# Forgetting branch, three of four head pairs: the second head's probabilities are turned through VectorE squares and DRAM too

## The chip, the cores and the metric

The kernel runs on one core of a Trainium2 chip. The metric is device time in microseconds (us) of one execution, as the median of three runs. One further execution was taken with the hardware profiler; the profile and the trace are of that one. Engines are named PE (TensorE), DVE (VectorE), ACT (ScalarE), POOL (GpSimd) and SP (SyncE). A line such as L1264 is line 1264 of the kernel before.

## What is computed

One layer of a decoder: an RMS norm, one input projection, three causal token mixers (A forgetting attention, B sparse attention with a top-k indexer, C dilated windows), each with its own gate, a merge, an output projection, the residual and a last norm. Sequence 1024, model width 1024, float32. The change touches mixer A (and, by a shared helper, a little of B's bookkeeping). Cut to A:

```
def forgetting_attention(q, k, v, log_f):
    scale = Dh ** -0.5
    c = jnp.cumsum(log_f, axis=1).transpose(0, 2, 1)
    ...
    def block(i):                      # 128 queries
        logits = jnp.einsum('bqhd,bkhd->bhqk', qb, k, preferred_element_type=F32) * scale
        logits = logits + (cb[..., :, None] - c[..., None, :])
        logits = jnp.where(kpos[None, :] <= qpos[:, None], logits, -jnp.inf)
        p = jax.nn.softmax(logits, axis=-1)
        return jnp.einsum('bhqk,bkhd->bqhd', p.astype(v.dtype), v)
```

A has 8 heads of 64 channels. A query block b (0 to 7) sees (b + 1) blocks of 128 keys.

## The kernel before

**Order of the work.** `build_plan` writes one list of steps by hand (kinds such as `logits`, `square`, `turn`, `exp`, `pv`, `block`). Each engine walks that same list and issues its own part of every step, in order, and semaphores tie the engines together. So what stands behind a waiting instruction in the list waits too, on that engine.

**Tiling of A.** Two heads make a chunk of 128 channels, the "channel" `ch` 0 to 3. In a channel the query blocks go in six runs: (0,1), (2,3), 4, 5, 6, 7, which see 3, 7, 5, 6, 7 and 8 key blocks of 128 for each head. `pair_run` lays the runs out as a pipeline over steps s:

1. `logits` of run s: PE multiplies queries by keys for both heads into PSUM slots (L1252); DVE adds the causal triangle and the forget bias and takes the row maximum (L1870, L1871).
2. `square` of run s (only where `by_dma` holds): ACT computes exp for the first head into `pa[:, 0]` (L1506). DVE transposes it in place with one STREAM_TRANSPOSE (L1792), which turns each 32 x 32 square of it but leaves the squares where they are.
3. `turn` of run s - 1: PE transposes what has not gone the other way, 128 x 128 at a time, against an identity (L1264), in groups of up to four to a PSUM bank; ACT copies each group to `pta` (L1537).
4. `exp` of run s: ACT computes exp for the second head (L1519), then issues the store of the first head's squares to a DRAM scratch (L1528). POOL issues four loads (L1036), one for each 32 partitions, which bring the squares back to where a full transpose has them, in one of the two tiles `ptsa`.
5. `pv` of an earlier run (3 steps back, `LAG`; 2 where the next run isn't `by_dma`): PE multiplies values by the turned probabilities of both heads (L1291), ACT copies the result to `ya` (L1554).
6. The rest of the step is filled with pieces of the next channel's projection, 12 matmuls of 512 columns a piece (`block`, L1118 to L1120). Two blocks of weights, with two such pieces each (one for each half of the 1024 tokens), make a tile q, k or v; when a half is done, ACT and DVE copy it out of its PSUM bank in two parts, high and low (`qa`, `ka`: L1483, L1814; `va`: L1805). Only then may PE claim that bank again.

`by_dma` holds in A for 17 of the 24 runs: all of channels 0 and 1 and all but the last of channel 2. In these 17 runs the first head goes through DVE and DRAM, the second through PE. The weights of a block go through SP's queue into `w_raw`, then ACT (L1355) and DVE (L1651) split them into `w_hl`, three blocks ahead. The two PSUM slots are freed by ACT's exps (`slot_free`); `logits` of a run wait for the slots of the run before.

**Places in time.** Channels 0 to 2 of A run from 611 to 774 us of the trace. The runs of channel 1 have their `logits` at 660.35, 671.93, 683.88, 693.35, 699.01 and 708.51 us.

## Time and profile before

| | us |
|---|---|
| median of 3 runs | 1348.44 (1348.2 to 1348.98) |
| the profiled execution itself | 1348.53 |
| its span, first to last instruction | 1346.7 |
| PE busy | 1326.0 (98%) |
| DVE busy | 771.0 (57%) |
| ACT busy | 629.4 (47%) |
| POOL busy | 264.1 (20%) |

The busy time of an engine is the union of its instructions; matmuls overlap one another, so a row's count times its mean is more than the time it takes on PE. What a group of matmuls takes is the distance from its start to the start of the next group. Idle time of an engine other than PE costs nothing by itself.

### The profile page before, as it was taken

To read this page: it belongs to the slowest core of one execution; us is meant where nothing else is said; L and a number is where in the kernel's file an instruction comes from. 1 tells how busy PE (TensorE), PEld (TensorE's weight loads), DVE (VectorE), ACT (ScalarE), POOL (GpSimd) and SP (SyncE) were. 2 spreads that over 40 slices of the span, in tenths; PEclk is the share of its full clock that TensorE was granted. 3 is DMA by queue.
4 is the path that set the end of the run, shared out by engine and by line. 5 is a ranking of instruction groups with operands and counts; after the bars stand their busy time and mean duration, and the time that the engine had idled before them with its cause. 6 is when DMAs were issued, how large, how long until landed. Compare 5 with 4: busy or idle time off the path is not lost.

```text
span 1346.7 us, 20780 instructions
## 1 busy us (share of the span) xinstructions
PE 1326.0 (98%) x7690; PEld 1082.1 (80%) x7690; DVE 771.0 (57%) x1716; ACT 629.4 (47%) x1381; POOL 264.1 (20%) x423
## 2 busy tenths in 40 slices
PE   7999999999999999999999999999999999999998
PEld 6988888777878888887788777787878788888886
DVE  6569866766766875565555555744445354233534
ACT  7467766766754541113443465644454322213223
POOL 3123211002103100003344313323332220000000
PEclk9999999999999999999999999999999999999999
DMA  7054222122214322225555423433544352222522
GB/s 227 24 141 126 71 63 72 50 53 73 72 41 119 99 64 82 80 72 163 162 153 155 141 87 105 127 92 84 156 127 124 119 161 55 78 78 63 188 100 96
DMA packets 146052, 139.54 MB, mean 104 GB/s; under 512 B 13888, under 2 KB 124096, under 8 KB 145696
## 3 DMA queue, kind: packets, MB, share of 16 engines
q0 software_dynamic: 22896, 67.42, 16.9%
q1 hardware_dynamic: 97824, 58.22, 16.0%
q10 hardware_dynamic: 25232, 12.59, 3.2%
q8 instruction: 62, 1.02, 0.3%
q14 instruction: 38, 0.31, 0.1%
HBM read 99.95 MB, written 34.03 MB: 99 GB/s over the span
## 4 chain that ended last, share of the span: by engine, by line
PE 95%; DVE 2%; ACT 1%; issue 1%; POOL 1%; DMA 0%; ACTq 0%; POOLq 0%; DVEq 0%
PE bank L1118 23%; PE bank L1120 23%; PE bank L1119 23%; PE bank L1291 6%; PE slot L1252 6%; PE bank L1264 5%; PE slot L1118 2%; PE slot L1119 2%; PE slot L1120 2%; PE slot L1226 1%; PE bank L1131 0%; DVE slot L1871 0%; ACT yc L1554 0%; DMA iq_st<-iq_hl 0%; PE bank L1177 0%
## 5 line engine op out<-in xcount | busy, mean ns | idle before, releaser
L1118 PE MATMUL bank<-hs,w_hl 128*128 128x512 f32 x1088 | 431.5, 397 | 0.7 <-DVE qa L1814 0.7
L1120 PE MATMUL bank<-hs,w_hl 128*128 128x512 f32 x1088 | 424.3, 390 | 0.0
L1119 PE MATMUL bank<-hs,w_hl 128*128 128x512 f32 x1088 | 423.8, 390 | 0.0
L1651 DVE TENSOR_TENSOR w_hl<-w_raw,w_hl 128x512 fp32r<-128x512 f32 (+1 forms) x168 | 113.6, 678 | 220.7 <-ACT w_hl L1355 219.2
L1120 PEld LDWEIGHTS bank<-hs,w_hl 128*128 128x128 f32 x1088 | 204.2, 188 | 44.0
L1118 PEld LDWEIGHTS bank<-hs,w_hl 128*128 128x128 f32 x1088 | 204.3, 188 | 43.6 <-issue 3.4
L1119 PEld LDWEIGHTS bank<-hs,w_hl 128*128 128x128 f32 x1088 | 204.6, 188 | 39.6
L1355 ACT ACTIVATE w_hl<-w_raw 128x512 fp32r<-128x512 f32 (+1 forms) x168 | 103.9, 621 | 165.1 <-PE bank L1120 155.9
L1678 DVE TENSOR_SCALAR_CACHE_REDUCE idle_out<-score,state 128x768 uint8<-128x768 f32 (+3 forms) x140 | 115.0, 822 | 4.0
L1871 DVE CUSTOM_DVE_ANT_0 slot<-slot,score 128x128 f32<-128x128 f32 (+5 forms) x64 | 47.0, 786 | 50.1 <-PE slot L1252 50.0
L1560 ACT ACTIVATE idle_out<-score,state 128x896 bf16<-128x896 f32 x64 | 69.9, 1093 | 10.0 <-DVE state L1674 8.8
L1036 POOL DMA_DIRECT2D ptsa<-square_scratch x68 | 48.3, 718 | 91.6 <-PE bank L1291 68.8
L1602 ACT ACTIVATE tm<-bank 128x512 f32<-128x512 f32 x46 | 27.5, 598 | 72.3 <-PE bank L1120 72.2
L1036 POOL DMA_DIRECT2D ptsb<-square_scratch x48 | 31.1, 654 | 79.4 <-DMA square_scratch<-pb 68.2
L1036 POOL DMA_DIRECT2D c_tables<-square_scratch x48 | 30.8, 648 | 65.9 <-DMA square_scratch<-pb 65.9
L1849 DVE SCALAR_TENSOR_TENSOR score<-relu_t,nat,score 128x1024 f32<-128x1024 f32 (+5 forms) x42 | 37.9, 947 | 5.0 <-ACT relu_t L1468 4.5
L1870 DVE TENSOR_TENSOR slot<-slot,tri_b 128x128 f32<-128x128 f32 x64 | 20.5, 320 | 33.7 <-PE slot L1252 33.1
L1519 ACT ACTIVATE share_b<-slot,c_tables 128x128 f32<-128x128 f32 (+1 forms) x96 | 38.6, 421 | 1.1 <-DVE c_tables L1871 0.9
L1871 DVE CUSTOM_DVE_ANT_0 slot<-slot,negc 128x128 f32<-128x128 f32 (+7 forms) x48 | 36.8, 766 | 1.7
L1291 PE MATMUL bank<-pta,va 128*64 128x128 f32 x376 | 36.6, 277 | 1.1 <-ACT pta L1537 1.1
L1554 ACT ACTIVATE yb<-bank 128x128 f32<-128x128 f32 (+1 forms) x24 | 7.5, 313 | 64.3 <-PE bank L1291 64.2
L1118 PE MATMUL bank<-ych,w_hl 128*128 128x512 f32 x96 | 37.3, 389 | 0.0
(338 smaller groups left out, 2415.1 us busy)
## 6 DMA issues: line engine op xcount, KB each, us to landing
w_raw<-in_w_in_dram SPq DMA_DIRECT2D x136, 256.0 KB, 2.9
merged_scratch<-ms POOLq DMA_DIRECT2D x16, 512.0 KB, 3.5
ms<-merged_scratch POOLq DMA_DIRECT2D x16, 512.0 KB, 4.0
square_scratch<-pb ACTq DMA_DIRECT2D x20, 256.0 KB, 2.3
xn<-in_x_dram SPq DMA_DIRECT2D x8, 512.0 KB, 6.6
iq_st<-iq_hl POOLq DMA_DIRECT2D x32, 128.0 KB, 2.8
w_raw<-in_w_o_dram SPq DMA_DIRECT2D x16, 256.0 KB, 4.0
v_scratch<-vtc POOLq DMA_DIRECT2D x6, 512.0 KB, 3.1
```

Of the source, the lines that this page charges most:

```text
L1036: pool.dma_start(PTQ[br][n % 2][32 * j:32 * j + 32, 0:W // P, :].rearrange("a b (i c) -> a (b i) c", i=4), mid[0:W // P, :, 32 * j:32 * j ...
L1118: pe.matmul(out_, wh, mh, start=start, stop=False)
L1119: pe.matmul(out_, wh, ml, start=False, stop=False)
L1120: return pe.matmul(out_, wl, mh, start=False, stop=stop)
L1252: ins = pe.matmul(slot_of(a, hh)[1][:, c0:c1], qt[qp][rows, tq], kt[kp][rows, first + c0:first + c1], start=n == 0, stop=n == 2)
L1264: ins = pe.transpose(bank[grp["use"][0]][:, j * P:(j + 1) * P], PR[u["br"]][:, row, at_col:at_col + P], ident[:])
L1291: ins = pe.matmul(bank[a["pv"][0]][cols, out], values, turned, start=c == 0, stop=c == n - 1)
L1355: A(dst, src, ACTF.Copy).then_inc(w_high, 1)
L1560: A(idle_out[:, 0:W], score_of(j + 2), ACTF.Sign, bias=cand[:, j:j + 1].bitcast(F32), scale=-1.0, accum_out=val[:, j:j + 1]).then_inc(act_ ...
L1651: v.tensor_tensor(lo, src, hi.bitcast(F32), ALU.subtract).then_inc(w_low, 1)
L1678: return v.tensor_scalar(idle_out8[:, 0:W] if W <= 6 * P else idle_out[:, 0:W], score_of(j + 2), cand[:, j:j + 1].bitcast(F32), None, op, ...
L1871: v.tensor_tensor_reduce(o, o, logit_bias(x, hh), -slope, 0.0, ALU.add, ALU.min, stats_of(x, hh)[0]).then_inc(logit_ready, 1)
```

## The change

In the 17 `by_dma` runs of A the second head goes the way of the first:

- `HEADS` says how many heads go through squares: 2 in A, 1 in B. `moved` now holds both heads' blocks, so `turn` has no groups for these runs.
- A new step `square_second` stands right behind `exp`: DVE transposes `pa[:, 1]` in place, waiting for ACT's exp of it, and ACT issues its store, waiting for that transpose.
- POOL issues the same four loads a run, each now of both heads' blocks, and waits for both stores.
- ACT's exp of the second head waits until the second store of the run before has landed (`second_stored`), since the store reads `pa[:, 1]`.
- The `ptsa` tiles are twice as large (16 blocks of 128, 8 KiB a partition) and lie at 36 and 44 KiB, the first of them where `pta` is; the first run that turns by PE again waits until the last `pv` from that tile is done. One `negc` tile moves from 48 to 76 KiB. There are four DRAM scratches instead of two, each twice as large.

The diff:

```diff
@@ -57,2 +57,3 @@
 SQUARED = {"a": 8, "b": 4}
+HEADS = {"c": 1, "a": 2, "b": 1}
 LAG = {"a": 3, "b": 2}
@@ -77,3 +78,3 @@
     count = {"ring": 0, "tp": 0, "hs": 0, "S": 0, "L": 0, "unit": 0, "z": 0, "zt": 0, "qk": 0, "taken": 0}
-    tiles, unit_of_tp, units_seen, last_split, last_taken, squares = {}, [], [], {}, {}, []
+    tiles, unit_of_tp, units_seen, last_split, last_taken, squares, goals = {}, [], [], {}, {}, [], [0, 0]
 
@@ -273,3 +274,5 @@
                     return
-                own = [(x["b"], 0, c) for x in runs[s] for c in range(x["W"] // P)]
+                own = [[(x["b"], hh, c) for x in runs[s] for c in range(x["W"] // P)] for hh in range(HEADS[br])]
+                goal, second = goals[len(squares) % 2], sum(y["br"] == "a" for y in squares)
+                goals[len(squares) % 2] += 64
                 at = len(squares) - 2
@@ -277,3 +280,4 @@
                     x.update(square=len(squares), single=sum(y["slots"] == 1 for y in squares),
-                             moved={part: k for k, part in enumerate(own[:SQUARED[br]])})
+                             moved={part: k for k, part in enumerate(part for parts in own for part in parts[:SQUARED[br]])},
+                             wide=min(len(own[0]), SQUARED[br]) * P, room=squares[-4]["goal"] if len(squares) > 3 else 0, goal=goal + 64, second=second)
                 step("square", unit=runs[s][-1], n=len(squares), before=squares[at] if at >= 0 else None)
@@ -303,2 +307,7 @@
                 plan.append(("exp", runs[s][-1]))
+                if by_dma[s] and br == "a":
+                    step("square_second", unit=runs[s][-1])
+                elif br == "a":
+                    for x in runs[s]:
+                        x["behind"] = squares[-1]
             x = runs[min(s, n - 1)][-1]
@@ -629,3 +638,3 @@
         PT = {br: at(k, f"pt{br}", [P, PTS[br], 4, P]) for br, k in (("c", 54), ("a", 36), ("b", 40))}
-        PTQ = {"a": [at(k, f"ptsa{k}", [P, TB, P]) for k in (44, 76)], "b": [at(46, "ptsb", [P, 4, P])]}
+        PTQ = {"a": [at(k, f"ptsa{k}", [P, 2 * TB, P]) for k in (36, 44)], "b": [at(46, "ptsb", [P, 4, P])]}
 
@@ -636,3 +645,3 @@
         bmc = at(62, "bmc", [P, 2, 2 * P])
-        negc = [at(k, f"negc{k}", [P, T]) for k in (64, 48, 52)]
+        negc = [at(k, f"negc{k}", [P, T]) for k in (64, 76, 52)]
         khb, qb, srow = at(80, "khb", [P, 2, T], F32R), at(88, "qb", [P, 2, 2, HALF], F32R), at(76, "srow", [P, T])
@@ -718,3 +727,4 @@
         square_in = [sem(f"square_in{i}") for i in range(2)]
-        square_dram = [nc.dram_tensor(f"square_scratch_{i}", [TB, P, P], F32, kind="Internal").ap() for i in range(2)]
+        squared_second, second_stored = sem("squared_second"), sem("second_stored")
+        square_dram = [nc.dram_tensor(f"square_scratch_{i}", [2 * TB, P, P], F32, kind="Internal").ap() for i in range(4)]
         v_dram = [nc.dram_tensor(f"v_scratch_{i}", [P, T], F32, kind="Internal").ap() for i in range(2)]
@@ -943,2 +953,10 @@
 
+            def load_square(u):
+
+                n, nb = u["square"], len(u["moved"])
+                for j in range(4):
+                    pool.dma_start(PTQ[u["br"]][n % 2][32 * j:32 * j + 32, 0:nb, :].rearrange("a b (i c) -> a (b i) c", i=4),
+                                   square_dram[n % 4][0:nb, :, 32 * j:32 * j + 32].rearrange("b (i a) c -> a (b i) c", i=4)
+                                   ).then_inc(square_in[n % 2], 16)
+
             k = 0
@@ -1029,4 +1047,3 @@
                 elif kind == "square":
-                    u, n, mid = a["unit"], a["n"], square_dram[a["n"] % 2]
-                    br, W = u["br"], len(u["moved"]) * P
+                    u, n = a["unit"], a["n"]
                     if a["before"] is not None:
@@ -1034,6 +1051,5 @@
                     pool.wait_ge(square_stored, 16 * (n + 1))
-                    for j in range(4):
-                        pool.dma_start(PTQ[br][n % 2][32 * j:32 * j + 32, 0:W // P, :].rearrange("a b (i c) -> a (b i) c", i=4),
-                                       mid[0:W // P, :, 32 * j:32 * j + 32].rearrange("b (i a) c -> a (b i) c", i=4)
-                                       ).then_inc(square_in[n % 2], 16)
+                    if u["br"] == "a":
+                        pool.wait_ge(second_stored, 16 * (u["second"] + 1))
+                    load_square(u)
                 elif kind == "stat_store":
@@ -1273,3 +1289,3 @@
                         if a["dma"]:
-                            pe.wait_ge(square_in[a["square"] % 2], 64 * (a["square"] // 2 + 1))
+                            pe.wait_ge(square_in[a["square"] % 2], a["goal"])
                         claim(pe, a["pv"])
@@ -1340,2 +1356,15 @@
 
+            def store_square(u, hh):
+
+                n, W = u["square"], u["wide"]
+                if hh:
+                    act.wait_ge(squared_second, u["second"] + 1)
+                else:
+                    act.wait_ge(squared, n + 1)
+                if u["room"]:
+                    act.wait_ge(square_in[n % 2], u["room"])
+                act.dma_start(square_dram[n % 4][hh * (W // P):(hh + 1) * (W // P)].rearrange("b p c -> p b c"),
+                              PR[u["br"]][:, hh, 0:W].rearrange("p (b c) -> p b c", c=P)
+                              ).then_inc(second_stored if hh else square_stored, 16)
+
             def split_high(upto):
@@ -1500,3 +1529,3 @@
                         act.wait_ge(square_stored, 16 * a["n"])
-                    if u["held"] is not None and any(part[1] == 0 for part in u["held"]["groups"][0]["parts"]):
+                    if u["held"] is not None and any(part[1] == 0 for grp in u["held"]["groups"][:1] for part in grp["parts"]):
                         full(act, u["held"]["groups"][0]["use"])
@@ -1511,3 +1540,6 @@
                     if a["held"] is not None:
-                        full(act, a["held"]["groups"][-1]["use"])
+                        for grp in a["held"]["groups"][-1:]:
+                            full(act, grp["use"])
+                        if a["held"]["dma"] and a["br"] == "a":
+                            act.wait_ge(second_stored, 16 * (a["held"]["second"] + 1))
                         if a["held"]["dma"] and not a["dma"]:
@@ -1523,8 +1555,5 @@
                     if a["dma"]:
-                        n, br, W = a["square"], a["br"], len(a["moved"]) * P
-                        act.wait_ge(squared, n + 1)
-                        if n >= 2:
-                            act.wait_ge(square_in[n % 2], 64 * (n // 2))
-                        act.dma_start(square_dram[n % 2][0:W // P].rearrange("b p c -> p b c"),
-                                      PR[br][:, 0, 0:W].rearrange("p (b c) -> p b c", c=P)).then_inc(square_stored, 16)
+                        store_square(a, 0)
+                elif kind == "square_second":
+                    store_square(a["unit"], 1)
                 elif kind == "turn":
@@ -1536,2 +1565,4 @@
                         turned_room(act, grp)
+                        if u["br"] == "a":
+                            full(act, u["behind"]["pv"])
                         A(PT[u["br"]][:, grp["tp"] % PTS[u["br"]], 0:n, :].rearrange("p c q -> p (c q)"), bank[b][:, 0:n * P],
@@ -1786,3 +1817,3 @@
                     u = a["unit"]
-                    W = len(u["moved"]) * P
+                    W = u["wide"]
                     if u["slots"] == 2:
@@ -1792,2 +1823,7 @@
                     v.transpose(PR[u["br"]][:, 0, 0:W], PR[u["br"]][:, 0, 0:W]).then_inc(squared, 1)
+                elif kind == "square_second":
+                    u = a["unit"]
+                    own = PR[u["br"]][:, 1, 0:u["wide"]]
+                    dve.wait_ge(slot_free, last_slot(u) + 1)
+                    v.transpose(own, own).then_inc(squared_second, 1)
                 elif kind in ("vc", "va"):
```

**What moves on ACT.** Channel 1, run (2,3): the exps of both heads, the store, the copy of the second half of `qa` out of PSUM and the next split of weights. Before:

```order
L1506 ACTIVATE pa,nat<-slot,nmax 128x384
L1506 ACTIVATE pa,nat<-slot,nmax 128x512
L1537 ACTIVATE pta<-bank 128x384
L1519 ACTIVATE pa,nat<-slot,nmax 128x384
L1519 ACTIVATE pa,nat<-slot,nmax 128x512
L1528 DMA square_scratch<-pa 128x7x128
L1483 ACTIVATE qa<-bank 128x512
L1355 ACTIVATE w_hl<-w_raw 128x512
```

and now:

```order
L1535 ACTIVATE pa,nat<-slot,nmax 128x384
L1535 ACTIVATE pa,nat<-slot,nmax 128x512
L1551 ACTIVATE pa,nat<-slot,nmax 128x384
L1551 ACTIVATE pa,nat<-slot,nmax 128x512
L1366 DMA square_scratch<-pa 128x7x128 x2
L1512 ACTIVATE qa<-bank 128x512
L1384 ACTIVATE w_hl<-w_raw 128x512
```

The copy of the turned group (`pta`) is gone, and a second store stands between the exps and the copy of `qa`.

**What moves on DVE**, at the same place: the last row maximum, the transposes of `pa` in place, the low half of `qa`, a split of weights. Before:

```order
L1871 ISA slot,nmax<-slot,negc 128x512
L1871 ISA nmax 128x1
L1792 STREAM_TRANSPOSE pa<-pa 128x896
L1814 SCALAR_TENSOR_TENSOR qa<-bank,qa 128x512
L1651 TENSOR_TENSOR w_hl<-w_raw,w_hl 128x512
```

and now:

```order
L1907 ISA slot,nmax<-slot,negc 128x512
L1907 ISA nmax 128x1
L1823 STREAM_TRANSPOSE pa<-pa 128x896
L1828 STREAM_TRANSPOSE pa<-pa 128x896
L1850 SCALAR_TENSOR_TENSOR qa<-bank,qa 128x512
L1682 TENSOR_TENSOR w_hl<-w_raw,w_hl 128x512
```

A second transpose stands ahead of the low half of `qa`.

**What moves on PE**, at the end of channel 2: the last of the `pv` products from `ptsa` and `pta` (of runs 5 and 6), the transposes of the run that isn't `by_dma`, and the logits of channel 3's first run. Before:

```order
L1291 MATMUL bank<-ptsa,va 64x128
L1291 MATMUL bank<-pta,va 64x128
L1291 MATMUL bank<-ptsa,va 64x128
L1291 MATMUL bank<-pta,va 64x128
L1264 MATMUL bank<-ident,pa 128x128 x8
L1252 MATMUL slot<-ka,qa 128x128 x6
L1252 MATMUL slot<-ka,qa 128x256 x6
L1264 MATMUL bank<-ident,pa 128x128 x8
```

and now:

```order
L1136 MATMUL bank<-hs,w_hl 128x512
L1307 MATMUL bank<-ptsa,va 64x128 x26
L1280 MATMUL bank<-ident,pa 128x128 x8
L1268 MATMUL slot<-ka,qa 128x128 x6
L1268 MATMUL slot<-ka,qa 128x256 x6
L1280 MATMUL bank<-ident,pa 128x128 x8
```

The 26 products are 12 of run 5 and 14 of run 6, and all read `ptsa`; no transposes stand between the projection's matmuls and the products of earlier steps any more.

## Rows read from the trace of the kernel before

**Rows 1.** The page, part 1: busy time of each engine.
```profile
PE 1326.0 (98%) x7690; PEld 1082.1 (80%) x7690; DVE 771.0 (57%) x1716; ACT 629.4 (47%) x1381; POOL 264.1 (20%) x423
```

**Rows 2.** Busy time by stage: stretch, length, engines, granted clock, DMA share, GB/s.
```profile
613.00:773.00 160.00, 158.73 (x1145) 127.21 (x1145) 89.24 (x193) 71.58 (x173) 65.42 (x90) 1.00 0.57 157
```

**Rows 3.** Groups by line, PE, the same stretch: count, busy, mean ns, idle before.
```profile
L1264 PE MATMUL bank<-ident,pa 128*128 128x128 f32 x100 | 15.4, 286 | 0.0
```

**Rows 4.** Timeline of PE, channel 1: start, duration, line; transposes and what follows.
```profile
675.20 0.55 PE L1264 MATMUL bank<-ident,pa 128*128 128x128 f32 x3
675.50 0.47 PE L1118 MATMUL bank<-hs,w_hl 128*128 128x512 f32 x1
...
686.95 0.99 PE L1264 MATMUL bank<-ident,pa 128*128 128x128 f32 x7
687.70 0.48 PE L1118 MATMUL bank<-hs,w_hl 128*128 128x512 f32 x1
...
695.41 0.89 PE L1264 MATMUL bank<-ident,pa 128*128 128x128 f32 x5
696.07 0.47 PE L1118 MATMUL bank<-hs,w_hl 128*128 128x512 f32 x1
...
717.36 1.10 PE L1264 MATMUL bank<-ident,pa 128*128 128x128 f32 x8
718.22 0.48 PE L1118 MATMUL bank<-hs,w_hl 128*128 128x512 f32 x1
```

**Rows 5.** Timeline, run (2,3), channel 0, then channel 1: ACT, DVE, PE.
```profile
625.18 1.11 DVE L1792 STREAM_TRANSPOSE pa<-pa 128x896 f32<-128x896 f32 x1
626.32 0.37 ACTq L1528 DMA_DIRECT2D square_scratch<-pa  x1
626.56 0.20 ACT L1519 ACTIVATION_READ_ACCUMULATOR pa<-slot,nmax 128x1 f32 x1
626.73 0.60 ACT L1483 ACTIVATE qa<-bank 128x512 fp32r<-128x512 f32 x1
628.20 0.47 PE L1118 MATMUL bank<-hs,w_hl 128*128 128x512 f32 x1 [0.74 <-DVE qa L1814]
...
678.80 0.60 ACT L1483 ACTIVATE qa<-bank 128x512 fp32r<-128x512 f32 x1
681.07 0.39 PE L1118 MATMUL bank<-hs,w_hl 128*128 128x512 f32 x1
```

**Rows 6.** Timeline, channel 1, run 5's second head and the next logits.
```profile
697.18 0.14 DVE L1871 DVE_READ_ACCUMULATOR2_ANT nmax<- 128x1 f32 x1
697.69 0.91 ACT L1519 ACTIVATE pa<-slot,nmax 128x768 f32<-128x768 f32 x1
699.01 0.50 PE L1252 MATMUL slot<-ka,qa 64*128 64x512 f32 x2
```

**Rows 7.** Timeline, end of channel 2; then POOL's load issues (ns); then landings (us).
```profile
766.50 2.98 POOL L1036 DMA_DIRECT2D ptsa<-square_scratch  x4 [6.47 <-PE bank L1291]
771.73 0.29 PE L1291 MATMUL bank<-ptsa,va 128*64 128x128 f32 x1 [0.52 <-ACT ya L1554]
...
L1036 POOL DMA_DIRECT2D ptsa<-square_scratch x4: 787/787/787, 664.1 to 666.4; - x4
L1036 POOL DMA_DIRECT2D ptsa<-square_scratch x4: 618/618/633, 675.6 to 677.4; - x4
...
ptsa<-square_scratch POOLq DMA_DIRECT2D x24, 112.0 KB, 2.9
ptsa<-square_scratch POOLq DMA_DIRECT2D x12, 48.0 KB, 2.2
square_scratch<-pa ACTq DMA_DIRECT2D x6, 448.0 KB, 3.7
```

**Rows 8.** DMA queues, 610 to 770 us: packets, MB, share of 16 engines.
```profile
q0 software_dynamic: 5018, 13.23, 30.1%
q10 hardware_dynamic: 13072, 6.55, 14.3%
```

## The prediction

> **What bounds the kernel now.** The page's first part comes first: PE is busy 98% of the span, no other engine above 57% [rows 1]. So an edit counts by what it does to PE's row of instructions: what leaves it, and where PE is made to wait. Second, the stage. The view by stage for the stretch that holds all 17 runs shows PE busy 158.73 of 160 us at a granted clock of 1.00, DVE 89.24, ACT 71.58, and the DMA engines at a share of 0.57 [rows 2]. The reader should see two things there: PE has 1.3 us of idle time to lose, and it is not the arithmetic engines but the DMA engines that come nearest to a second bound. Third, the groups by line: the transposes that go are 100 of L1264, with no idle time ahead of them [rows 3]. Fourth, the timelines around the places where PE's next instruction depends on what ACT, DVE or POOL will now do later.
>
> **What is removed on PE.** A group's price is the distance to the next group's start. Three transposes take 0.30 us, five 0.66, seven 0.75, eight 0.86 [rows 4]; for six I take 0.74, just under seven. A channel has groups of 3, 7, 5, 6, 7 and 8: 0.30 + 0.75 + 0.66 + 0.74 + 0.75 + 0.86 = 4.06 us. Three channels less the last eight: 12.2 - 0.86 = 11.3 us. (The mean of 286 ns in rows 3 times 100 would give 28.6; it counts overlap twice.) The products themselves stay as many, 200 from `ptsa` now being 400. ACT loses 31 copies of turned groups; since ACT is not the bound this is worth nothing but where the next paragraphs use it.
>
> **What is added on DVE and ACT.** DVE gets 17 transposes of up to 1.2 us (896 columns: 1.11) [rows 5], about 17 us on 89 busy of 160 [rows 2]: room enough. But the engines are in order, and ACT now waits for DVE's second transpose before it can issue the second store. What stands behind that wait, in run (2,3), is ACT's copy of the second half of `qa`, then DVE's low half; only then may PE claim the bank for the next tile's second half.
>
> In channel 0 the trace shows this chain already binding. The second exp's last part ends at 626.56 + 0.20 = 626.76; ACT's copy of `qa` begins at 626.73; PE resumes at 628.20 after 0.74 idle, released by DVE `qa` [rows 5]. So the chain from the copy's start to PE is 1.47 us. Now the second transpose comes between: 626.76 + 1.11 = 627.87, then the store's issue, which ACT shows as 0.37 [rows 5] and which may or may not hold the next copy back. The copy starts 1.15 to 1.55 us later; I take 1.4. PE, which would have been there 0.30 sooner, resumes 1.4 later: 1.7 us of the 11.3 are lost. In channel 1 the copy starts at 678.80, so the bank was free at 680.27 and PE came at 681.07 [rows 5], not waiting. Now the bank is free at 681.67 and PE would come at 680.77: 0.9 lost, and as much in channel 2. Together 3.5 us; bounds 2.8 (issue free) to 4.2 (0.37 each time, and a DVE start 0.1 late).
>
> **Logits that wait for the exp.** Run 6's logits follow run 5's after one piece of projection only. In channel 1 the second exp starts at 697.69, lasts 0.91 and its last part; PE's logits start at 699.01 [rows 6], with almost no slack. Taking five transposes (0.66) out lets PE come at 698.35. The exp can start sooner too, since ACT has no `pta` copy ahead of it: the row maximum is ready at 697.18 + 0.14 = 697.32 [rows 6], so with 0.1 to start it gains 0.27. The slot is freed 0.27 sooner, PE would be 0.66 sooner: 0.4 lost, in three channels 1.2 us (0 if the exp's end leaves more slack than I see; 2.0 if the exp gains nothing).
>
> **The end of channel 2.** Run 6 there is the last `by_dma` run, and its `pv` stands directly behind run 5's, two steps back instead of three. Its loads cannot be issued before run 4's `pv` has released the `ptsa` tile. Let S = 766.50 be the first issue. PE starts run 6's `pv` at 771.73, after 0.52 idle [rows 7]. The view names ACT for that idle time, but the last of the four issues is at S + 2.2 and takes 2.9 to land, which is 771.6: it was the load. Now each issue carries 14 blocks instead of 7. The issue takes 618 ns for 3 blocks and 787 for 8 [rows 7], 33.8 a block, so 990 for 14: the last begins at S + 2.97. It takes 2.2 us for 48 KB to land and 2.9 for 112 KB [rows 7]; the same slope gives 4.1 for 224 KB. Landed at S + 7.1. PE without waiting would be there at 771.73 - 0.52 - 0.75 = S + 3.96. It waits 3.1 where it waited 0.52: 2.6 us lost. Bounds: 1.4 (a landing no longer than the 2.9 of today) to 5 (the second store of run 6 landing late, or the loads slowed by 2.4).
>
> The Trainium skill, "DMA: Bandwidth & Descriptors", section on the anatomy of a DMA on the gpsimd path, fits such a transfer as 2.0 us plus bytes over 436 GB/s. For 224 KB this is 2.5 us, and the sum would end 1.6 us lower. The trace disagrees already at 112 KB, where the fit says 2.3 and the row 2.9, so the row's slope is used.
>
> **Elsewhere the loads are hidden.** In the full pipeline two `pv` lie between release and use. The narrowest such distance, two steps with one and two pieces of projection, is some 11 to 12 us after the transposes are gone; loads of 16 blocks need 0.4 + 3 x 1.06 + 4.4 = 8 us. So 3 us or more are left. Of the second stores, run 5's stands nearest to the exp that waits for it. Run 5's second exp ends near 698.7, its transpose a us later, and a store of 448 KB takes 3.7 us [rows 6, 7]: landed by 703.4. Run 6's second exp can't start before its logits of 699.01 are done and DVE has taken two row maxima of over a us each, about 703.5 to 704 by my estimate; and PE's next logits come another 4 us later. No cost, if transfers take what they take today.
>
> **Sum.** 11.3 - 3.5 - 1.2 - 2.6 = 4.0 us less. The profiled execution took 1348.53, 0.09 above the median: 1348.5 - 4.0 = **1344.5 us**. About 0.2% (2.7 us) is what a measurement of this kernel can tell from no change; so faster begins at 1345.7 and slower at 1351.1.
>
> **The rivals.**
>
> *The DMA engines become the bound (slower).* The stores' queue took 6.55 MB at a share of 14.3%, nearly all squares; both stores make that 28.6%. The loads are about as many MB of POOL's queue, 13.23 MB at 30.1% [rows 8], so 14.9% more. The stage's share goes from 57% to 86%, in a stretch that is also some us shorter. For it: above that mean there will be bursts in which stores, loads, `va` and weights queue behind one another, and every one of the slacks above is a latency. Against it: 86% is still below one, and no more than one step's transfers can be late before the next step's wait for them. It decides from where transfers take some 3 us longer than now. Priced at 4 us longer (twice today's): the wait at the end of channel 2 grows by 4; run 5's and run 6's exps, and so the next logits, come 1 us late twice in each channel, 6; the loads of two runs a channel are 1 us late, 6 less one for the start of channel 0, where nothing is under way yet, 5. The 15 us on 1344.5 would be 1359.5, and half of them, if only the wider runs are hit, 1352; with the mean below one I take **1354**. The Trainium skill, "DMA: Bandwidth & Descriptors", section on queues and arbitration, has each engine go round its queues packet by packet; then a store isn't kept behind all queued loads, and the mechanism would be the milder for it.
>
> *The waits give it all back (no change).* As my forecast, but ACT is held by 0.4 for every issue, the chain over `qa` costs 4.2, the logits 2.0, the last load 5: 11.3 - 11.2 leaves nothing. For it: what the profile shows of each of the three is a latency with others behind it. Against it: these are three upper bounds at once. **1348.4**.
>
> *Nearly all of it arrives (faster).* If ACT's store does not delay the copy of `qa` beyond what other waits cover, and the last load lands in 3 us: 11.3 - 2.8 - 0 - 1.4 = 7.1, so **1341.4**. For it: ACT and DVE both have over 40% idle time in the stage. Against it: the chain over `qa` was already binding in channel 0.
>
> **Chances.** My forecast 0.47 (its own range 1342.5 to 1347), DMA-bound 0.18, all given back 0.23, nearly all of it 0.12. Of my own case 0.36 lie below 1345.7 and 0.11 above; with the last rival faster has 0.48. Same: 0.11 + 0.22 + 0.03 = 0.36. Slower: 0.16. The range from 1341 to 1353 leaves out the far half of the first rival and little on the low side.
>
> **What would show it.** Right: L1264's count on `pa` falls by 100; PE idle before the third piece in run (2,3) of about 2.4, 0.9 and 0.9 us, released by DVE `qa`; about 0.4 us before run 6's logits, released by ACT's exp; one wait of about 3 us between the two last `pv` from `ptsa`; DMA share of the stage near 0.85; other PE idle of the stage below 1 us. Wrong: PE waiting in front of `pv` in the middle of a channel, exps released by `square_scratch` stores before PE waits on them, landings of 6 us or more (the first rival); no idle time at `qa` (the last one); or a granted clock below 1.00 in the stretch, which no term here has.

## The result and the profile after

The changed kernel takes **1365.43 us** (1364.82 to 1365.99), the kernel before 1348.42 beside it: ratio (after over before) 1.0127, 95% interval 1.0114 to 1.014. It is 17 us slower where 4 us faster was forecast. The profiled execution has a span of 1364.1 us, 17.4 more than before.

The busy times by engine, and the groups of the stage that answer to [rows 1, 3]:

```profile
PE 1322.0 (97%) x7590; PEld 1076.5 (79%) x7590; DVE 783.7 (57%) x1733; ACT 617.5 (45%) x1350; POOL 276.7 (20%) x423
```

```profile
L958 POOL DMA_DIRECT2D ptsa<-square_scratch x68 | 61.6, 914 | 83.5 <-DMA square_scratch<-pa 67.9 <-PE bank L1307 15.6
L1134 PE MATMUL bank<-hs,w_hl 128*128 128x512 f32 x141 | 58.9, 418 | 6.3 <-DVE qa L1850 6.3
...
L1307 PE MATMUL bank<-ptsa,va 128*64 128x128 f32 x400 | 27.7, 291 | 10.8 <-issue 10.8
...
L1268 PE MATMUL slot<-ka,qa 64*128 64x512 f32 (+3 forms) x234 | 25.0, 347 | 5.2 <-ACT pa L1551 3.8 <-ACT pa L1535 1.3
...
L1551 ACT ACTIVATE pa<-slot,nmax 128x1024 f32<-128x1024 f32 (+7 forms) x25 | 18.8, 754 | 27.0 <-DMA square_scratch<-pa 23.9 <-DVE nmax L1907 3.1
```

PE has lost exactly the 100 transposes. What replaced them stands after the second bar: PE idles 6.3 us at `qa`, 5.2 us ahead of logits and 10.8 us ahead of `pv`. The view calls the last "issue", but the sequencer waits there on `square_in`, the loads. Behind those waits stand POOL, which waits 67.9 us for stores before it may load, and ACT, which waits 23.9 us for stores before the second exp.

The stage, in a window 20 us longer than that of [rows 2]: busy us (and instructions) of PE, PEld, DVE, ACT and POOL, then granted clock, DMA share, GB/s.

```profile
613.00:793.00 180.00, 157.61 (x1071) 123.72 (x1070) 102.33 (x209) 61.70 (x145) 82.14 (x94) 0.96 0.85 214
```

The queues and landings that answer to [rows 7, 8], 610 to 790 us. The first row is the DMA engines' busy share, in tenths, in 40 slices; the last column of the last three rows is the median time from issue to landing, in us:

```profile
DMA  6586959397798939999798959992999999977993
...
q0 software_dynamic: 6832, 20.45, 45.7%
q10 hardware_dynamic: 26144, 13.11, 25.7%
...
square_scratch<-pa ACTq DMA_DIRECT2D x12, 448.0 KB, 5.2
ptsa<-square_scratch POOLq DMA_DIRECT2D x24, 224.0 KB, 5.7
w_raw<-in_w_in_dram SPq DMA_DIRECT2D x18, 256.0 KB, 6.5
```

The mean share of 0.85 is what the prediction expected, but it is made of slices at 90% and more (the nines) with gaps between. In this stretch a 448 KB store lands in 5.2 us (median) where it took 3.7, and a 224 KB load in 5.7 where 4.1 was assumed.

**Where PE's time went.** I compared each distance from one group's start to the next with the same distance in the kernel before. The stage is 17.7 us longer although 11.3 us of transposes are gone, so 29.0 us were lost:

| place (three channels) | forecast loss | measured loss |
|---|---|---|
| at `qa` in run (2,3), with the slow matmuls behind | 3.5 | 9.3 |
| logits of run 6 | 1.2 | 0.6 |
| logits of run 7 (behind the second exp of run 6) | 0 | 3.8 |
| logits of the next channel's first run | 0 | 1.6 |
| `pv` in mid-channel, with the slow matmuls behind | 0 | 5.3 |
| the two last `pv` from `ptsa`, end of channel 2 | 2.6 | 8.4 |

Three timelines show the links. First channel 0, run (2,3), which answers to [rows 5]:

```profile
627.52 0.37 ACTq L1366 DMA_DIRECT2D square_scratch<-pa  x1
627.93 0.60 ACT L1512 ACTIVATE qa<-bank 128x512 fp32r<-128x512 f32 x1 [1.59 <-DVE pa L1828]
628.56 0.69 DVE L1850 SCALAR_TENSOR_TENSOR qa<-bank,qa 128x512 fp32r<-128x512 f32 x1 [1.07 <-ACT qa L1512]
629.40 0.47 PE L1134 MATMUL bank<-hs,w_hl 128*128 128x512 f32 x1 [2.63 <-DVE qa L1850]
...
630.62 0.63 PE L1135 MATMUL bank<-hs,w_hl 128*128 128x512 f32 x1
631.04 0.63 PE L1136 MATMUL bank<-hs,w_hl 128*128 128x512 f32 x1
```

The chain is the one forecast, and its wait nearly so (2.63 for 2.4). Not forecast is what follows: matmuls of 0.63 us that start 0.43 apart. The windows show the granted clock:

```profile
631.00:634.00 3.00, 3.00 (x10) 2.07 (x8) 0.00 (x0) 0.00 (x0) 0.96 (x1) 0.57 0.67 161
640.00:643.00 3.00, 3.00 (x29) 2.17 (x28) 2.41 (x5) 1.58 (x4) 0.00 (x0) 1.00 0.70 202
```

PE is busy in all 3 us of the first window, at 0.57: mostly the lower level, 1.2 GHz, against 2.4 in the second. The three pieces around the wait took 12.88 us, where three undisturbed pieces take 8.38: 2.6 of wait and 1.9 of slow matmuls.

Second, the turn of channel 0 to 1, ACT and its queue:

```profile
666.12 0.37 ACTq L1366 DMA_DIRECT2D square_scratch<-pa  x1
...
674.33 0.37 ACT L1551 ACTIVATE pa<-slot,nmax 128x128 f32<-128x128 f32 x1 [5.34 <-DMA square_scratch<-pa]
...
687.08 0.47 PE L1134 MATMUL bank<-hs,w_hl 128*128 128x512 f32 x1 [2.76 <-DVE qa L1850]
```

The second store of run 7 (512 KB) is issued at 666.12, and the exp that needs its buffer starts 8.2 us later. Everything behind it on ACT and DVE is late, and some thirteen microseconds further on PE waits 2.76 us at `qa`, where 0.9 was forecast.

Third, the end of channel 2, which answers to [rows 7]:

```profile
764.12 0.37 ACTq L1366 DMA_DIRECT2D square_scratch<-pa  x1
...
771.69 1.01 ACT L1551 ACTIVATE pa<-slot,nmax 128x896 f32<-128x896 f32 x1 [2.88 <-DMA square_scratch<-pa]
...
772.24 3.66 POOL L958 DMA_DIRECT2D ptsa<-square_scratch  x4 [7.61 <-DMA square_scratch<-pa]
...
773.97 0.37 ACTq L1366 DMA_DIRECT2D square_scratch<-pa  x1
...
779.41 3.92 POOL L958 DMA_DIRECT2D ptsa<-square_scratch  x4 [3.51 <-DMA square_scratch<-pa]
...
782.15 1.53 PE L1307 MATMUL bank<-ptsa,va 128*64 128x128 f32 x24 [3.42 <-issue]
...
787.59 3.18 PE L1307 MATMUL bank<-ptsa,va 128*64 128x128 f32 x28 [3.90 <-issue]
```

Run 5's second store is issued at 764.12. ACT's second exp of run 6 and run 5's loads both wait for it, until 771.69 and 772.24. So run 6's second store is issued only at 773.97, and its loads wait for that one until 779.41. Before, these loads waited for a `pv` to free the tile; now they wait for the second store. Two `pv` wait, not one.

### The profile page after: what moved, and what is told of

Same layout as the page of the kernel before. It is cut to its first block, busy times and chain, and to the rows that moved or that the text cites. A ratio compares the mean times of both kernels' runs of the same rounds, so it can differ in the third digit from the quotient of the medians.

```text
span 1364.1 us, 20548 instructions
## 1 busy us (share of the span) xinstructions
PE 1322.0 (97%) x7590; PEld 1076.5 (79%) x7590; DVE 783.7 (57%) x1733; ACT 617.5 (45%) x1350; POOL 276.7 (20%) x423
## 4 chain that ended last, share of the span: by engine, by line
PE 86%; DMA 4%; DVE 4%; ACT 2%; issue 2%; POOL 1%; ACTq 0%; POOLq 0%; DVEq 0%
PE bank L1134 22%; PE bank L1136 21%; PE bank L1135 21%; PE bank L1307 5%; PE slot L1268 5%; PE bank L1280 4%; DMA square_scratch<-pa 3%; PE slot L1134 2%; PE slot L1135 2%; PE slot L1136 2%; DVE slot L1907 1%; DMA ptsa<-square_scratch 1%; PE slot L1242 1%; DVE pa L1828 1%; PE bank L1147 0%
## 5 line engine op out<-in xcount | busy, mean ns | idle before, releaser
L958 POOL DMA_DIRECT2D ptsa<-square_scratch x68 | 61.6, 914 | 83.5 <-DMA square_scratch<-pa 67.9
L1551 ACT ACTIVATE pa<-slot,nmax 128x1024 f32<-128x1024 f32 (+7 forms) x41 | 30.5, 750 | 29.4 <-DMA square_scratch<-pa 23.9
L1268 PE MATMUL slot<-ka,qa 64*128 64x512 f32 (+3 forms) x312 | 33.3, 347 | 5.2 <-ACT pa L1551 3.8
L1307 PE MATMUL bank<-ptsa,va 128*64 128x128 f32 x400 | 27.7, 291 | 10.8 <-issue 10.8
```

Source lines behind the costliest of these rows:

```text
L958: pool.dma_start(PTQ[u["br"]][n % 2][32 * j:32 * j + 32, 0:nb, :].rearrange("a b (i c) -> a (b i) c", i=4), square_dram[n % 4][0:nb, :, 32 ...
L1268: ins = pe.matmul(slot_of(a, hh)[1][:, c0:c1], qt[qp][rows, tq], kt[kp][rows, first + c0:first + c1], start=n == 0, stop=n == 2)
L1307: ins = pe.matmul(bank[a["pv"][0]][cols, out], values, turned, start=c == 0, stop=c == n - 1)
L1551: ins = A(PR[x["br"]][:, hh, x["col"]:x["col"] + x["W"]], slot_of(x, hh)[1], ACTF.Exp, bias=mx, scale=-1.0, accum_out=dn)
```

## The experiments

**Theory A:** the extra bytes keep the DMA engines full in bursts, transfers land some us later, and each latency that was just hidden shows. **Theory B:** it is the order on the engines: ACT and POOL wait for one more transpose and one more store, whatever the bytes.

### Bytes taken out, waits left

`e1_light` keeps every instruction and wait of the changed kernel; the second store moves one block, and the loads bring the first head's blocks only. `e2_stores` halves the loads alone. Both compute the second head's products from the first head's squares.

```
-  moved={part: k for k, part in enumerate(part for parts in own for part in parts[:SQUARED[br]])},
+  moved={part: k for parts in own for k, part in enumerate(parts[:SQUARED[br]])},
-  n, nb = u["square"], len(u["moved"])
+  n, nb = u["square"], u["wide"] // P
   (e1_light alone, in store_square)
+  m = P if hh else W
```

> The changed kernel with all its instructions and waits, but with little more traffic than before: the second store carries one block of 128 only, and the four loads bring the first head's squares alone, which the second head's products then read too (so the second head's output is not the reference's). Theory A, the DMA engines are the bound: the landings fall back to 3 to 4 us, the waits for stores and loads go, and what is left is my own sum without the long last load: 1341 to 1346 us. Theory B, the order of waits itself (ACT behind the second transpose, the exp behind the second store) costs whatever the bytes: 1360 us or more. Theory C, the lower clock after long waits is a cost of its own: it goes with the waits, so it can only be seen here as granted clock back at 1.00 between 613 and 790 us.

> The changed kernel with its second stores in full, but the loads bring the first head's squares alone, read by both heads' products (the second head's output is not the reference's). Theory A: about half of the added bytes are gone; loads and stores are about as many MB, so about half of the 17 us, 1350 to 1356. If it is the stores and their own queue that make the exps late: 1356 to 1363. If the loads did it all: 1341 to 1347, with second stores landing in 4 us or less. Theory B: 1360 or more.

Measured: `e1_light` 1345.02 us (ratio 0.9976, 0.9967 to 0.9986), `e2_stores` 1348.52 (1.0002, 0.9992 to 1.0012), against 1365.43 with all bytes. With the waits in place and the bytes gone, 20 us come back: 17 for half of the loads, and then 3.5 more for nearly half of the stores. (In the other order the shares might be others; that was not run.) `e2_stores` came in between two of its expectations, just above "the loads did it all", with second stores landing in 3.9 us. The stage and landings of `e1_light`:

```profile
613.00:793.00 180.00, 172.22 (x1239) 136.18 (x1239) 112.13 (x239) 74.67 (x179) 71.18 (x97) 0.98 0.58 161
```

```profile
square_scratch<-pa ACTq DMA_DIRECT2D x6, 448.0 KB, 3.3
ptsa<-square_scratch POOLq DMA_DIRECT2D x24, 112.0 KB, 3.0
```

`e1_light` comes near the forecast, 3.3 us faster than before for a forecast of 4.0, but it isn't the kernel that was forecast: its loads are half as large. Two differences cancel in part: a shorter last load, and slow matmuls that the forecast did not price. Its trace has the waits at `qa` (2.60, 0.93, 0.93), 0.2 ahead of run 6's logits, one of 2.01 between the last two `pv`, and none in mid-channel.

### Bytes added to the kernel before

`e6_bytes` doubles each store of the forgetting branch into a scratch that nothing uses, and adds four loads a step of up to four blocks from it. `e10_b_loads` has only the loads, from the true scratch, `e11_b_stores` only the stores. The order of steps stays, but waits are added too. In both runs with added loads, POOL issues them ahead of the true ones; in `e6_bytes` alone it first waits for the added store. ACT's next exp of the first head waits for the added store in `e6_bytes` and `e11_b_stores`.

```
   (the loads as in e10_b_loads, the store as in e11_b_stores, both shortened)
+  pool.dma_start(spare[32 * j:32 * j + 32, 0:m, :]..., mid[0:m, :, 32 * j:32 * j + 32]...).then_inc(dummy_in, 16)
+  act.dma_start(dummy_dram[n][0:W // P]..., PR[br][:, 0, 0:W]...).then_inc(dummy_stored, 16)
```

> The kernel before, its transposes on PE as they were, with traffic added and nothing else: each of the 17 stores is issued twice, the second time to a scratch of its own, and four more loads a run bring up to four blocks of that scratch to a place nobody reads (so stores doubled, loads up by somewhat over a half). ACT waits for the added store before it overwrites the first head. Theory A: the landings rise to 5 us and more and PE waits for exps, logits and products: 1352 to 1362. Theory B: no new chain of waits that matters, 1348 to 1350.

> The kernel before, with four more loads a step of up to four blocks from the same scratch into a free place, issued ahead of the true ones; nothing reads them. No second stores. The run with both extra stores and these loads took 1360.4, 12 above before. Theory 'loads cost more than stores': 1355 to 1360. Rival 'the extra time was in the stores and in ACT's waits for them': 1348 to 1351.

> The kernel before, with every store of the forgetting branch's squares issued twice, the second into a scratch that nothing reads; ACT waits for both before it writes the tile again. No extra loads. Theory 'loads cost more than stores': 1349 to 1353. Rival 'the stores': 1356 to 1360.

Measured: both 1360.37 (1.009, 1.0074 to 1.0105); loads alone 1353.03 (1.0037, 1.0023 to 1.0051); stores alone 1350.27 (1.0013, 1.0004 to 1.0023). Transfers that nothing reads, with the waits that come with them, cost 12.0 us, about twice 4.5 + 1.7 (each against the kernel before beside it). `e10_b_loads` missed both of its expectations, between them. The true 112 KB loads of `e6_bytes` land in 4.9 us, in the kernel before in 2.9. The stage's share is 0.80 in `e6_bytes`; with the loads alone 0.67, with the stores alone 0.69:

```profile
613.00:793.00 180.00, 169.19 (x1223) 135.23 (x1223) 91.84 (x209) 76.66 (x187) 114.31 (x165) 0.99 0.80 211
```

```profile
613.00:793.00 180.00, 175.43 (x1293) 140.55 (x1291) 96.52 (x218) 81.98 (x202) 114.67 (x165) 1.00 0.67 178
```

These times are not of bytes alone: the added loads also take POOL time (114.67 busy against 71.52 in the same stretch of before). At the end of channel 2 `e10_b_loads` issues the added loads at 766.43, where before had the true ones at 766.50, and the true ones 2.6 us later. PE loses 3.2 us at this place, most of the 4.5. In `e6_bytes` it loses 7.2 of the 12 there:

```profile
765.98 0.60 ACTq L1551 DMA_DIRECT2D dummy_scratch<-pa  x1
...
773.59 2.58 POOL L1044 DMA_DIRECT2D spare<-dummy_scratch  x4 [4.86 <-issue]
...
781.62 0.45 PE L1304 MATMUL bank<-ptsa,va 128*64 128x128 f32 x1 [5.83 <-DMA ptsa<-square_scratch]
```

The added store is issued at 765.98, POOL begins its added loads at 773.59 and the true ones at 776.16, almost ten us later than before. It is a slow store with a wait behind it, as in the changed kernel. That wait stands in neither of the single runs, so the surplus of the 12.0 over 6.2 isn't shown to come from the bytes.

### Bytes or pieces

`e8_rows` reads the same blocks in rows of 512 bytes instead of pieces of 128, so they lie untransposed.

```
-  ...[32 * j:32 * j + 32, 0:nb, :].rearrange("a b (i c) -> a (b i) c", i=4), square_dram[n % 4][0:nb, :, 32 * j:32 * j + 32]...
+  ...[32 * j:32 * j + 32, 0:nb, :], square_dram[n % 4][0:nb, 32 * j:32 * j + 32, :].rearrange("b p c -> p b c")
```

> The changed kernel, but the loads of the forgetting branch read their blocks in rows of 128 values (512 bytes) where they read pieces of 32 values (128 bytes): the same bytes, the same four loads a step, the blocks then lie untransposed, so the output is not the reference's. Theory 'bytes': what costs is the bytes on the DMA engines; 1361 to 1369, landings of the 224 KB loads stay at 5 to 6.5 us, the stage's DMA share stays at 0.80 or more. Rival 'pieces': what costs is the number of short pieces a load is made of (four times as many); 1345 to 1352, share below 0.75 and landings of 3 to 4 us.

Measured: 1367.78 (1.0136, 1.012 to 1.0151), share 0.82, 224 KB loads landing in 5.0 us, 448 KB stores in 6.1. A quarter of the pieces buys nothing, so the length of the pieces isn't the cause. Nor is POOL's time to issue the larger loads: here an issue takes 620 ns on average, less than the 716 of `e2_stores` and the 914 of the changed kernel, and nothing comes back. What remains of the difference between `e2_stores` and the changed kernel is the bytes. The Trainium skill, "DMA: Bandwidth & Descriptors", section "Specifications", wants 512 bytes a transfer for line rate. By that rule the longer rows should have been the cheaper form. This stage, with 128 bytes against 512, doesn't bear it out.

### The order at qa

`e3_qa_first` is the changed kernel with the second transpose and store of run (2,3) moved behind the copies of `qa`. `e9_qa_light` makes the same move in `e1_light`.

```
+  late = []
+  for i, (kind, a) in enumerate(plan):
+      if kind == "square_second" and len(a["unit"]["run"]) == 2 and a["unit"]["b"] == 3:
+          late.append(i)
+  for i in reversed(late):
+      to = next(j for j in range(i, len(plan)) if plan[j][0] == "qa")
   ...
+      plan.insert(to, plan.pop(i))
```

> The changed kernel, but in run (2,3) of each channel the second transpose and the second store stand behind ACT's and DVE's copies of the second half of the next query tile. PE waited there 2.63, 2.76 and 0.96 us and ran some 4 us longer at the lower clock behind the first two. If that chain is a cost of its own: 7 to 10 us faster than the changed kernel, 1355 to 1358. Theory A in its strong form, where the DMA engines have no room left: what is gained at this place comes back as later landings, 1361 to 1366.

> The run with few bytes (second store of one block, loads of the first head's blocks only) together with the moved second store of run (2,3): second transpose and second store stand behind the copies of qa. The output is not the reference's. It prices the chain over qa without the bytes. The light run's trace has 2.6, 0.9 and 0.9 us of waits at qa, and in the first of them the matmuls behind the wait ran at the lower clock for about 2 us. Theory 'the wait chain costs by itself, and the slow matmuls come with the wait': 5 to 7 us faster than the light run, 1338 to 1340.5, no piece of projection behind qa over 9 us. Rival 'it comes back elsewhere, at the next exp, as it did with all bytes': 1342.5 to 1345.

Measured: with all bytes 1362.35 (1.0103, 1.0088 to 1.0118), 3 us better than the changed kernel. With few bytes 1339.43 (0.9929, 0.9914 to 0.9944), 5.6 us better than `e1_light`. Both waits at `qa` in channels 1 and 2 are gone there, and the one in channel 0 is 1.02 with the clock at 1.00 behind it. In `e3_qa_first` too the `qa` waits fell to 1.02, 1.15 and 1.14, but another store is now waited for, run 4's second. Channel 1, the second exp of run 5 and the logits of run 6:

```profile
690.53 0.37 ACTq L1374 DMA_DIRECT2D square_scratch<-pa  x1
...
699.68 0.90 ACT L1559 ACTIVATE pa<-slot,nmax 128x768 f32<-128x768 f32 x1 [3.13 <-DMA square_scratch<-pa]
...
700.72 2.61 PE L1276 MATMUL slot<-ka,qa 64*128 64x512 f32 x12 [2.91 <-ACT pa L1559]
```

Stores of 320 KB, which landed in 3.8 us (median) in the changed kernel, take 7.5 here, and PE waits at the next logits instead. In this stage, at a DMA share of 0.87, moving a transfer moved the wait.

### Loads in two sets

`e12_split` loads the first head's blocks after the first store and the second head's after the second: eight loads a step, bytes the same.

```
+  load_square(u, 0, u["wide"] // P)
   pool.wait_ge(second_stored, 16 * (u["second"] + 1))
+  load_square(u, u["wide"] // P, len(u["moved"]))
```

> The changed kernel with eight loads a step instead of four: the first head's blocks are loaded as soon as the first store has landed, the second head's after the second. Bytes the same, twice as many loads (each 0.6 to 0.8 us of POOL). Theory 'late start': the transfers bunch because the loads wait for the second store; spread out they land earlier, 1355 to 1362. Rival 'the bytes themselves, in whatever order': 1363 to 1370.

Measured: 1362.4 (1.0091, 1.0065 to 1.0117; single runs from 1356.65 to 1363.07). 3 us better than the changed kernel, in the gap between the two theories. In its profiled execution the 448 KB stores land in 7.5 us instead of 5.2, and PE waits 7.08 us ahead of the last `pv`. The loads start earlier, the stores land later; that the one causes the other is not shown.

### Four blocks of each head

`e14_four` takes at most four blocks of each head, 46 a channel against 36 before and 72 after, with the tiles where they lay before. `e15_four_qa` adds the move of `e3_qa_first`. (The 38, 29 and 58 blocks in the first expectation are miscounted: a channel's six runs have 36 blocks a head, and PE loses 10 transposes a channel, not 9.)

```
-SQUARED = {"a": 8, "b": 4}
+SQUARED = {"a": 4, "b": 4}
```

> The changed kernel with at most four blocks of each head by DMA (eight a step against up to sixteen, 38 a channel against 29 in the kernel before and 58 in the changed one); PE transposes the rest. The tiles lie where they lay in the kernel before. PE loses 9 transposes a channel, some 3 us in all. Theory 'the price follows the bytes': with 31% more blocks than before a fifth to a third of the 20 us, plus the chain over qa: 1350 to 1356. Rival 'the second store and its waits cost whatever its size': no better than the changed kernel, 1360 or more. Rival 'only bytes beyond some share cost': 1346 to 1349.

> The run with four blocks of each head by DMA (1349.7) and the moved second store of run (2,3) together: all outputs as the reference has them, 38 blocks a channel. In the four-block run the pieces behind the qa waits took 12.39, 9.19 and 9.19 us against 8.38 undisturbed. Theory 'with the bytes held near the old ones, the chain over qa is the rest of the price': 4 to 6 us faster than without the move, 1344 to 1346, so faster than the kernel before. Rival 'it comes back at the next exp, as with all bytes (3 of an expected 7 to 10 came)': 1347 to 1350.

Measured: 1349.72 (1.0011, 1.0001 to 1.0021), just under the first expectation's 1350 to 1356, and **1345.7** (0.9985, 0.9976 to 0.9994). The second computes everything and is 2.2 us below the 1347.88 of before beside it, a small gain. Its stage, and its landings:

```profile
613.00:793.00 180.00, 177.19 (x1319) 142.17 (x1319) 104.30 (x244) 83.61 (x202) 75.27 (x97) 1.00 0.65 177
```

```profile
square_scratch<-pa ACTq DMA_DIRECT2D x28, 256.0 KB, 3.2
ptsa<-square_scratch POOLq DMA_DIRECT2D x56, 128.0 KB, 3.3
```

At a share of 0.65 the loads of 128 KB land in 3.3 us (3.6 in the kernel before), the move at `qa` brings 4 us, and the clock stays at 1.00. PE keeps 0.93 us of wait in channel 0 and 0.83 at the end of channel 2.

## Why the prediction was wrong

**Right.** The 11.3 us of transposes: `e9_qa_light` has 2.3 us of new waits left (0.3 at `qa`, 0.6 at run 6's logits, 1.4 at the end of channel 2) and is 9.1 us below before, and 11.3 - 2.3 is 9.0. The chain over `qa` (2.4, 0.9, 0.9 forecast; 2.60, 0.93, 0.93 in `e1_light`). The stage's DMA share of 0.85. Run 6's logits were costed at 1.2 and lost 0.6, half of it. That `e1_light` ends within a us of the forecast is partly luck. With its loads of 7 blocks the prediction's own working gives a wait of some 1.1 at the end of channel 2, and 2.0 were measured; and slow matmuls, which no term has, took 1.9 at `qa`.

**The step that failed** is "Elsewhere the loads are hidden", with its condition "if transfers take what they take today". The condition was written down and the share that breaks it was worked out two paragraphs on. But each slack was then compared with a landing taken from a trace at a share of 0.57. Loads of 224 KB took 5.7 us, not the 4.1 of the slope, and stores 5.2, not 3.7; run 5's second store in channel 2, which this step counted as hidden, was waited for until 7.6 us after its issue. The step also counts the loads' slack from the `pv` that frees their tile, though the loads now wait for the second store as well: POOL's wait ahead of them, put down to stores, went from 14.9 us in the kernel before to 67.9. The same latency error sits in the sum twice more: the end of channel 2 lost 8.4 for a forecast of 2.6, since its loads now wait for a late store and not for a `pv`, and `qa` in channel 1 waited 2.76 for 0.9. `e1_light` against the changed kernel shows what the added bytes cost in all, these two places included: 20.4 us.

**The rival had the mechanism.** Its argument against itself, that 86% is still below one, was the wrong use of a mean: 23 of the forty slices between 610 and 790 us were at nine tenths and above. Its full price, 15 us, was near in size: 6 us of logits (5.4 measured), 5 of mid-channel loads (5.3), 4 more at the end (5.8). The places fit less well, so part of that is luck. Run 6's logits lost less than the forecast had, run 7's lost 3.8 and those of the next channel 1.6; the mid-channel loads were late at two places, not five, with slow matmuls behind one of them. Halving the price because the mean was below one had no row behind it. Missing in it was the chain over `qa`, which lost 5.8 beyond the forecast, part of it through exps held up by stores and part through the clock.

**Not in any term:** the clock. In `e1_light`, with few bytes, the three pieces around the 2.60 us wait took 4.46 us too long, 1.9 of it slow matmuls. I had listed a lower clock as a sign of error and given it no price.

**Still open.** `e2_stores` and the changed kernel differ in the size of the loads alone, 17 us. How much of that is the loads' own landing and how much their effect on the stores, for which ACT and POOL wait, is not taken apart. `e6_bytes` gives 12 us for fewer added bytes (20.52 MB on POOL's queue over 190 us, against 22.78) where taking bytes out gave 20, and it has waits of its own. So no run has the bytes of the changed kernel without waits for the added stores. That bytes and waits are both needed for the full price, by putting late stores and loads into PE's path, is read from the traces and was not tried by itself.

## What to carry to other kernels

When a change doubles the bytes of transfers, read every landing time again as if from the new DMA share: slacks measured at a share of 0.57 did not hold at 0.85, while the five runs at 0.65 to 0.69 stayed within 5 us of the kernel before. Look at the slices, not at the mean alone. Count a slack from the last thing that the transfer waits for. Here trading PE work for DMA work paid only in a small portion: 46 blocks a channel instead of 72 gave back 16 us, and mending the order then made it 2.2 us faster than before.

## What the hardware showed that I had not expected

**Landings grow before the mean share is near one.** A 112 KB load took 2.9 us at a share of 0.57, 3.9 in `e10_b_loads` at 0.67 and 4.9 in `e6_bytes` at 0.80. With the stores doubled and the loads as before (0.69, `e11_b_stores`) it still took 2.9. I had thought of the load as a threshold that is passed or not.

**A short wait can cost more than its length.** Behind waits of 2.63 and 2.76 us at `qa` the granted clock fell, and the matmuls after them started 0.43 us apart instead of 0.23. In `e1_light` and `e9_qa_light`, same place:

```profile
631.00:634.00 3.00, 3.00 (x11) 2.14 (x12) 0.00 (x0) 0.00 (x0) 2.93 (x4) 0.71 0.61 155
```

```profile
631.00:634.00 3.00, 3.00 (x22) 2.47 (x19) 2.09 (x5) 0.83 (x2) 2.86 (x4) 1.00 0.65 168
```

The first comes behind a wait of 2.60 us, the second behind one of 1.02. In the changed kernel the waits of 0.96 to 1.42 us were followed by no slow matmuls. But the length of the wait doesn't settle it: the clock was at 1.00 behind waits of 2.79 us at `qa` (`e8_rows`, channel 2), 2.09 at `qa` (`e6_bytes`, channel 1) and 3.69 at the last `pv` (`e10_b_loads`), while one of 2.23 at `qa` in `e14_four` had seven slow spacings behind it. What decides between them, these runs don't show. At channel 0's `qa` in the changed kernel a wait of 2.6 us cost 4.5. The Trainium skill, "TensorE: Matmul & The Clock Gate", section "Wait — 56ns, not 53.3ns?", gives the spacing of matmuls of 512 columns as 427 ns at the lower level and 216 at the upper one. The rows here agree at the lower level (0.43 us) and are a little longer at the upper one (0.23).
